# Full attention of a hybrid decoder step: scores from stacked high and low halves, a ring of two heads, six cache copies moved

## The chip, the cores and the metric

The kernel runs on one core of a Trainium2 chip. The metric is the time of one execution on the device in microseconds (us), lower is better. All data is float32 in memory. "float32r" in the profile (fp32r) is a rounded form of float32 in which TensorE works faster; a value split into a rounded high part and the rest as a low part keeps nearly all of its digits.

## The reference, cut to what matters

One layer of a decoder trunk for 1024 prompt rows and 8 x 8 sample rows. A projection gives queries, keys and values for four attentions: a full (differential) attention "B" with 4 heads, and three windowed ones. The change touches the full attention over the prompt alone, and the order of some copies of old cache rows to the output.

```python
qb = rms_norm(qb.reshape(b, s, B_HEADS, 2, HEAD_DIM), q_norm_b)      # 4 heads, 2 maps, 64 wide
kb = rms_norm(kb.reshape(b, s, B_HEADS, 2, HEAD_DIM), k_norm_b)
scores = jnp.einsum('bqhcd,bkhcd->bhcqk', q, k) * (d ** -0.5)        # c: the two maps
scores = scores - slopes[:, None, None, None] * rel.astype(jnp.float32)
p, _ = softmax_with_lse(scores, rel >= 0)                            # causal
a = p[:, :, 0] - lam * p[:, :, 1]
return jnp.einsum('bhqk,bkhe->bqhe', a, v)                           # v is 128 wide
```

## The kernel before, in words

The program is written out by hand: every engine has its own instruction list, and semaphores order them. In order of time there are 12 blocks of the input projection (kinds q, k, v for G = 0 to 3; G = 0 is the full attention B, G = 1 to 3 the windowed ones). After the three blocks of a G comes its attention over the prompt. Then come the sample rows together with the gates (902 to 1420 us), the two projections, and the output.

A block (`block_`) has nine row tiles: 8 of 128 prompt rows and one of the 64 sample rows. The weights of the next block are fetched meanwhile into a ring of four raw buffers by SyncE (SP, `load_chunk`), rounded by ScalarE (`split_hi`), and their low parts made by GpSimd (POOL, `split_lo`). `load_chunk` of a chunk waits until the one four before it has been split.

Queries and keys are normalised, stored to DRAM in 32 x 32 turned blocks, and read back as head dimension by row (`load_turned`, 16 transfers of 128 KB for each of qT and kT; those of q in the k block, those of k in the first four steps of the v block). qT and kT hold [128, 4 x 1024]: one head (64 dimensions of each map below each other) per 1024 columns.

The attention B of head h and query tile i is an element e = 8h + s, with i from TILE_ORDER (7, 0, 6, 1, 5, 2, 4, 3); it needs i + 1 key tiles. In turn:

- POOL (`scaled`): two multiplications of 64 x 128 put the scaled query of each map into its own half of qz; the other half of qz is zero (two memsets, `pad_first`), so that one product over 128 rows gives one map's scores. The first eight elements are made in the v block ahead of its second step's weight split, the others behind the scores of the element eight before.
- PE (`scores`): the product qz x kT in float32, both maps; later `probs_turn` (transposes) and `values`.
- VectorE (DVE): `biased` adds the bias table tB from PSUM and keeps the minimum; `combined` takes map 2 times lambda from map 1.
- ScalarE (ACT): `Exp`, `piece_move`, and `out_move`, which puts the result into the place of the used query in qT.
- SP: after the last weight split of the v block it loads the bias tables of heads 0 and 1 (`table_b`, since tB lies where raw does), then the tables of the later heads with four cache copies each (`tables`), and at the end four stores of 512 KB of qT to o_scr (`attention_out`).

SP issues in order: what it waits for holds back everything behind it. A cache copy (`copy_cache`, up to 2 MB) waits until the copy two before it has landed. There are 48 copies: 16 in attention B, 2 in the v block of each windowed group, 19 in the windowed attentions, 7 in the output.

## Time and profile before

| | us |
|---|---|
| median of 3 runs | 1657.69 (1652.74 to 1667.01) |
| the profiled execution's own time | 1662.27 |
| its span | 1660.3 |
| blocks of B: v block | 130 to 176 |
| attention B | 176 to 290 |
| output stage | 1550 to 1660 |

Busy time over the span: PE 1601.6 us, DVE 758.0, POOL 699.3, ACT 564.6. The profile gives start times in us from the span's start. A row of the timeline that says "x4" has merged four like instructions of an engine. A float32 matmul appears as two records, a float32r one as one. "SPq" is the issue of a transfer on SP, and its length is the time that the issue took.

### The profile page before, as it was taken

The numbers are of one execution on the slowest core, as the hardware profiler recorded it, in microseconds if no ns is written. First come the engines' busy times: TensorE is split into PE (matmuls) and PEld (weight loads), VectorE is DVE, ScalarE is ACT, GpSimd is POOL, SyncE is SP. The second block draws the span as 40 slices with busy tenths as digits, with TensorE's granted clock in tenths as the row PEclk, the third lists the DMA queues.
The fourth block names the chain that finished last, engine by engine and source line by source line (L and its number), as shares of the span: only waits on it lengthen the run. The fifth ranks groups of instructions, "written<-read, shape, count | busy, mean of one in ns | idle before, by whom it ended". The sixth has DMA issues, their size and how long they took to land.

```text
span 1660.3 us, 37307 instructions
## 1 busy us (share of the span) xinstructions
PE 1601.6 (96%) x14616; PEld 1374.4 (83%) x14616; DVE 758.0 (46%) x1852; ACT 564.6 (34%) x1341; POOL 699.3 (42%) x958
## 2 busy tenths in 40 slices
PE   6999999999999999999999999999999899999998
PEld 5787677878899999999999877778787688888787
DVE  5532577333473333733335544335454433588411
ACT  5321477121362123712136234334343234411300
POOL 5676340466533666446666112122121121675500
PEclk9999999999999999999999999999999999999999
DMA  5359896338983279933797889889988978865692
GB/s 162 112 147 189 275 310 220 102 85 155 268 274 91 83 164 255 307 104 105 169 276 246 282 304 313 276 299 324 320 297 300 306 255 248 290 199 166 206 330 95
DMA packets 351487, 369.84 MB, mean 223 GB/s; under 512 B 164113, under 2 KB 208274, under 8 KB 351314
## 3 DMA queue, kind: packets, MB, share of 16 engines
q1 hardware_dynamic: 306354, 308.55, 61.4%
q10 hardware_dynamic: 44960, 58.92, 10.6%
q8 instruction: 117, 1.92, 0.5%
q14 instruction: 56, 0.46, 0.1%
HBM read 310.83 MB, written 143.85 MB: 274 GB/s over the span
## 4 chain that ended last, share of the span: by engine, by line
PE 79%; DMA 5%; POOL 4%; DVE 4%; issue 2%; ACT 2%; SPq 1%; ACTq 1%; POOLq 0%; DVEq 0%
PE ps L2069 13%; PE ps L2071 13%; PE ps L2070 13%; PE ps L2122 4%; PE ps L2224 4%; PE ps L2123 4%; PE ps L2124 4%; PE ps L2281 4%; PE ps L2170 3%; PE ps L2244 3%; DMA v_in<-in_cache_a_kv 3%; PE ps L2342 3%; PE ps L2231 2%; PE ps L2191 2%; POOL rs L1047 2%
## 5 line engine op out<-in xcount | busy, mean ns | idle before, releaser
L1066 POOL TENSOR_TENSOR w_lo<-raw,w_hi 128x512 fp32r<-128x512 f32 x140 | 181.6, 1301 | 407.8 <-ACT w_hi L1276 407.3
L2069 PE MATMUL ps<-w_hi,hT 128*128 128x512 f32 x824 | 333.3, 405 | 2.1 <-POOL hT L1053 1.0
L2071 PE MATMUL ps<-w_hi,hT 128*128 128x512 f32 x824 | 330.0, 401 | 0.0
L2070 PE MATMUL ps<-w_lo,hT 128*128 128x512 f32 x824 | 329.8, 400 | 0.0
L2122 PE MATMUL ps<-w_hi,hT 128*128 128x256 f32 x768 | 225.6, 294 | 4.9 <-issue 4.6
L2069 PEld LDWEIGHTS ps<-w_hi,hT 128*128 128x128 f32 x824 | 206.4, 250 | 22.7 <-issue 1.4
L2071 PEld LDWEIGHTS ps<-w_hi,hT 128*128 128x128 f32 x824 | 206.0, 250 | 20.5
L2070 PEld LDWEIGHTS ps<-w_lo,hT 128*128 128x128 f32 x824 | 206.6, 251 | 19.4
L2123 PE MATMUL ps<-w_lo,hT 128*128 128x256 f32 x768 | 217.6, 283 | 0.0
L2124 PE MATMUL ps<-w_hi,hT 128*128 128x256 f32 x768 | 217.1, 283 | 0.1
L1120 POOL TENSOR_SCALAR qz<-qT,qcol 64x128 f32<-64x128 f32 x256 | 156.6, 612 | 109.6 <-PE ps L2170 54.4
L1276 ACT ACTIVATE w_hi<-raw 128x512 fp32r<-128x512 f32 x158 | 98.7, 628 | 282.7 <-DMA raw<-in_w_in 228.5
L2122 PEld LDWEIGHTS ps<-w_hi,hT 128*128 128x128 f32 x768 | 147.9, 193 | 12.0 <-issue 11.3
L2123 PEld LDWEIGHTS ps<-w_lo,hT 128*128 128x128 f32 x768 | 148.0, 193 | 1.6 <-issue 1.6
L2124 PEld LDWEIGHTS ps<-w_hi,hT 128*128 128x128 f32 x768 | 147.5, 192 | 0.0
L1796 DVE STREAM_TRANSPOSE k_in<-k_in 128x512 f32<-128x512 f32 x224 | 139.0, 678 | 5.2 <-DMA k_in<-in_cache_a_kv 2.9
L1047 POOL TENSOR_TENSOR rs<-ss,half_pow 128x8 f32<-128x8 f32 (+3 forms) x81 | 127.1, 1570 | 6.7
L1668 DVE TENSOR_TENSOR zn<-ps,rs 128x512 f32<-128x512 f32 (+1 forms) x72 | 49.8, 691 | 146.9 <-POOL rs L1047 146.9
L1386 ACT ACTIVATE sA<-sA,st_sum 128x128 f32<-128x128 f32 (+1 forms) x192 | 86.2, 449 | 59.9 <-DVE st_sum L1762 53.9
L1330 ACT ACTIVATE ps<-ps 128x512 f32<-128x512 f32 (+1 forms) x72 | 41.8, 580 | 180.0 <-PE ps L2071 171.6
L1653 DVE TENSOR_REDUCE ss<-ps 128x8 f32<-128x512 f32 (+1 forms) x72 | 49.7, 690 | 116.4 <-ACT ps L1330 116.4
L2224 PE MATMUL ps<-kT,qz 128*128 128x128 f32 (+1 forms) x384 | 100.4, 348 | 1.0 <-issue 0.8
(229 smaller groups left out, 2763.6 us busy)
## 6 DMA issues: line engine op xcount, KB each, us to landing
out<-in_cache_a_kv SPq DMA_DIRECT2D x32, 2040.0 KB, 13.9
k_in<-in_cache_b_kv SPq DMA_DIRECT2D x128, 256.0 KB, 4.3
v_in<-in_cache_b_kv SPq DMA_DIRECT2D x128, 256.0 KB, 6.3
raw<-in_w_in SPq DMA_DIRECT2D x104, 256.0 KB, 3.3
k_in<-in_cache_a_kv SPq DMA_DIRECT2D x104, 256.0 KB, 8.4
v_in<-in_cache_a_kv ACTq DMA_DIRECT2D x96, 256.0 KB, 7.2
out<-in_cache_a_kv SPq DMA_DIRECT2D x8, 2016.0 KB, 9.9
raw<-in_w_in ACTq DMA_DIRECT2D x40, 256.0 KB, 6.8
```

The source lines that it names most:

```text
L1047: return pool.tensor_tensor(out, in_, half_pow[0:r, 0:heads], ALU.pow)
L1066: pool.tensor_tensor(lo, raw_of(q), hi.bitcast(F32), ALU.subtract).then_inc(lo_done, 1)
L1120: return pool.tensor_scalar(qz[rows, half, cols], qT[rows, c * SEQ + i * P:c * SEQ + (i + 1) * P], qcol[rows, (0 if G else 1):(0 if G else ...
L1276: act.activation(weights(q)[0], raw_of(q), ACT.Copy).then_inc(hi_done, 1)
L1796: dve.transpose(k_in[:, gg % NKS, j, :], k_in[:, gg % NKS, j, :]).then_inc(s_kt, 1)
L2069: pe.matmul(z, hi, wh, start=first, stop=False)
L2070: pe.matmul(z, hi, wl, start=False, stop=False)
L2071: return pe.matmul(z, lo, wh, start=False, stop=last)
L2122: pe.matmul(part, hi, wh, start=k == 0, stop=False)
L2123: pe.matmul(part, hi, wl, start=False, stop=False)
L2124: ins = pe.matmul(part, lo, wh, start=False, stop=k == KC - 1)
L2224: pe.matmul(bank(s % 4)[:, 0:W], qz[:, hh, i * P:(i + 1) * P], kT[:, k0:k0 + W], start=True, stop=True).then_inc(aq, 1)
```

## The change

- Scores: the two products are float32r. k_hl holds, for one map of one head, the rounded keys in partitions 0 to 63 and their low parts in 64 to 127. q_hi holds the rounded query twice (in both halves), q_lo its low part twice. Scores = q_hi x k_hl + q_lo x k_hl. A piece narrower than 256 columns is widened to 256.
- For that each head and map takes 1024 columns in both halves, so qT and kT hold two heads and are a ring. One head's keys are 8 transfers of 128 KB, its queries 8 as well. Heads 0 and 1 are loaded where all four were; head h + 2 when head h has been scored, in SP's list at the fourth element of head h.
- POOL: `query_parts` (two multiplications and a subtraction of 128 x 256) replaces `scaled` for G = 0; `key_parts` (two rounds of a cast and a subtraction of 64 x 512, and a cast of 64 x 1024) is new, once per head and map. In the v block steps 1 to 4 have two `query_parts` each, steps 5, 6, 7 a `key_parts` each, all ahead of the step's weight split. The memsets of qz for G = 0 go.
- The output of B goes to a ring of four tiles, oB, and is stored per element (64 KB) by SP; `out_move` waits for the store of the element four before.
- Cache copies: 10 instead of 16 in B, 3 instead of 2 in each of three v blocks, 10 instead of 7 in the output stage.

```diff
-COPIES_B, COPIES_A = 16, ((2, 2, 2, 2), (2, 2, 2, 1), (1, 1, 1, 1))
-COPIES_V, COPIES_OUT = 2, 7
+COPIES_B, COPIES_A = 10, ((2, 2, 2, 2), (2, 2, 2, 1), (1, 1, 1, 1))
+COPIES_V, COPIES_OUT = 3, 10
...
+            def load_head(kind, part):
+                h, rest = divmod(part, 8)
+                mp, d, j = rest // 4, rest // 2 % 2, rest % 2
...
+                p0, c0 = HD * d + 32 * j, head_at(h, mp)
+                out = (kT if kind == "k" else qT)[p0:p0 + 32, c0:c0 + SEQ]
...
+            def attention_b_io():
+                more_copies(2)
+                for e in range(32):
+                    h, s = divmod(e, 8)
+                    if s == 3 and h < 2:
+                        sp.wait_ge(*scored_heads(h + 1))
+                        sp.wait_ge(bs, 16 + 16 * (h + 1))
+                        for kind, loaded in (("k", kt_in), ("q", qt_in)):
+                            sp.wait_ge(loaded, turned_in_dram(0, h + 1))
+                            for part in range(8 * h + 16, 8 * h + 24):
+                                load_head(kind, part)
+                        table_b(h + 2)
+                    sp.wait_ge(bo, 8 + e + 1)
...
+                    sp.dma_start(o_scr[0][i * P:(i + 1) * P, h * P:(h + 1) * P], oB[:, e % 4, :])\
+                        .then_inc(sig_in[e % 4], 16)
+                    if s == 4:
+                        more_copies((COPIES_B - 2) // B_HEADS)
...
+                    if kind == "v" and 0 < at_ < 5 and G == 0:
...
+                        for n in range(2 * at_ - 2, 2 * at_):
+                            query_parts(n)
+                    if kind == "v" and 4 < at_ < NT and G == 0:
+                        key_parts(0, at_ - 5) if at_ < 7 else key_parts(1, 0)
...
+            def query_parts(e):
+                h, i = e // 8, TILE_ORDER[e % 8]
+                if h:
+                    pool.wait_ge(bq, 16 + 2 * (e - 8) + 2)
...
+                pool.tensor_scalar(hi_q, raw_q, qcol[:, 1:2], None, ALU.mult)
+                link(pool.tensor_scalar(raw_q, raw_q, qcol[:, 1:2], None, ALU.mult))
+                pool.tensor_tensor(lo_q, raw_q, hi_q.bitcast(F32), ALU.subtract).then_inc(qz_ready, 1)
+
+            def key_parts(h, mp):
+                pool.wait_ge(kt_in, turned_in_dram(0, max(h, 1)))
+                pool.wait_ge(*lo_ready(last_split[0]))
+                pool.wait_ge(qz_ready, 8 * max(h, 1) + (mp if h > 1 else 0))
+                for x0 in range(head_at(h, mp), head_at(h, mp) + SEQ, CW):
+                    cols = slice(x0, x0 + CW)
+                    link(pool.tensor_copy(k_hi[HD:P, :], kT[HD:P, cols]))
+                    link(pool.tensor_tensor(k_hl[HD:P, cols], kT[HD:P, cols], k_hi[HD:P, :].bitcast(F32), ALU.subtract))
+                whole = slice(head_at(h, mp), head_at(h, mp) + SEQ)
+                pool.tensor_copy(k_hl[0:HD, whole], kT[0:HD, whole]).then_inc(h_lo, 1)
...
+                key_parts(1, 1)
+                for e in range(8, 32):
+                    h, s = divmod(e, 8)
+                    if h > 1 and s < 2:
+                        key_parts(h, s)
+                        pool.wait_ge(qt_in, turned_in_dram(0, h))
+                    query_parts(e)
...
+                    if e % 8 == 0:
+                        pe.wait_ge(h_lo, SPLIT_0 + 2 * h + mp + 1)
...
-                        w = min(CW, W - w0)
-                        ins = pe.matmul(ps[:, mp * 1024 + w0:mp * 1024 + w0 + w],
-                                        qz[:, mp, s * P:(s + 1) * P], kT[:, ds(h * SEQ + w0, w)],
-                                        start=True, stop=True)
+                        w = min(CW, max(2 * P, W - w0))
+                        z, keys = ps[:, mp * 1024 + w0:mp * 1024 + w0 + w], k_hl[:, k0 + w0:k0 + w0 + w]
+                        pe.matmul(z, q_hi[:, mp, s * P:(s + 1) * P], keys, start=True, stop=False)
+                        ins = pe.matmul(z, q_lo[:, k0 + s * P:k0 + (s + 1) * P], keys, start=False, stop=True)
```

POOL in the v block of G = 0, before (w_lo is the low part of the next block's weights, qz the padded query):

```order
L1066 TENSOR_TENSOR w_lo1_74<-raw_70,w_hi1_73 128x512
L1130 MEMSET qz_85 64x1024
L1131 MEMSET qz_85 64x1024
L1120 TENSOR_SCALAR qz_85<-qT_75,qcol_54 64x128 x16
L1066 TENSOR_TENSOR w_lo1_74<-raw_70,w_hi1_73 128x512 x7
```

Of the change, the end of the same block (k_hi is a scratch row for the rounded keys; the eight query parts of three instructions each stand ahead, two for each of the first four of these splits):

```order
L1114 TENSOR_TENSOR w_lo1_74<-raw_70,w_hi1_73 128x512
L1199 CAST k_hi_89<-kT_76 64x512
L1200 TENSOR_TENSOR k_hl_88<-kT_76,k_hi_89 64x512
L1199 CAST k_hi_89<-kT_76 64x512
L1200 TENSOR_TENSOR k_hl_88<-kT_76,k_hi_89 64x512
L1202 CAST k_hl_88<-kT_76 64x1024
L1114 TENSOR_TENSOR w_lo1_74<-raw_70,w_hi1_73 128x512
```

The 16 short multiplications stood in one run ahead of seven splits; now 24 instructions of 256 columns and three groups like this one stand between the splits, and the last split comes behind all of them.

SP from the end of the v block to the end of attention B, before (tB the bias table, out the cache copies, o_scr the stored result):

```order
L828 DMA tB_97<-in_bias_b 128x1024 x2
L818 DMA out_5<-v_sb_77 128x512
L713 DMA out_6<-in_cache_a0_kv 16x15x512
L713 DMA out_7<-in_cache_a1_kv 16x63x512
L713 DMA out_8<-in_cache_a2_kv 16x48x680 x4
L713 DMA out_6<-in_cache_a0_kv 16x15x512
L713 DMA out_7<-in_cache_a1_kv 16x63x512
L828 DMA tB_97<-in_bias_b 128x1024
```

The same place of the change:

```order
L862 DMA tB_102<-in_bias_b 128x1024 x2
L852 DMA out_5<-v_sb_77 128x512
L732 DMA out_6<-in_cache_a0_kv 16x15x512
L732 DMA out_7<-in_cache_a1_kv 16x63x512
L902 DMA o_scr0<-oB_95 128x128 x3
L795 DMA kT_76<-blocks_scr0k 32x32x32 x8
L795 DMA qT_75<-blocks_scr0q 32x32x32 x8
L862 DMA tB_102<-in_bias_b 128x1024
L902 DMA o_scr0<-oB_95 128x128 x2
L732 DMA out_8<-in_cache_a2_kv 16x48x680 x2
```

Sixteen transfers for head 2 now stand between the stores of elements 2 and 3, and the same for head 3 eight elements on.

## Rows read from the trace of the kernel before

**Rows 1.** The page's fourth part: the chain that ended last, by engine.
```profile
PE 79%; DMA 5%; POOL 4%; DVE 4%; issue 2%; ACT 2%; SPq 1%; ACTq 1%; POOLq 0%; DVEq 0%
```
**Rows 2.** Window of B's second head: length, busy PE, PEld, DVE, ACT, POOL; clock, DMA.
```profile
204.60:232.10 27.50, 27.50 (x159) 20.11 (x158) 20.79 (x57) 19.83 (x52) 10.68 (x16) 1.00 0.92 302
```
**Rows 3.** Waits from 120 to 292 us: who for whom, total, times, longest.
```profile
DVE rlB L1716 <- ACT sB L1371: 8.7, 9, 1.1
```
**Rows 4.** Timeline of PE: float32 scores, then the float32r products of a block.
```profile
204.80 1.88 PE L2170 MATMUL ps<-kT,qz 128*128 128x512 f32 x4
206.52 0.61 PE L2191 MATMUL ps<-v_sb,ptB 128*128 128x128 f32 x4
...
172.95 0.40 PE L2069 MATMUL ps<-w_hi,hT 128*128 128x512 f32 x1
173.42 0.40 PE L2071 MATMUL ps<-w_hi,hT 128*128 128x512 f32 x1
```
**Rows 5.** Groups of POOL by shape: busy us, mean ns of one, idle before.
```profile
L1120 POOL TENSOR_SCALAR qz<-qT,qcol 64x128 f32<-64x128 f32 x256 | 156.6, 612 | 109.6 <-PE ps L2170 54.4 <-PE ps L2224 39.8
L1174 POOL COPY q_rep<-qTs 32x64 f32<-32x64 f32 x128 | 29.6, 232 | 27.2 <-issue 11.2 <-PE ps L2286 10.3
L1174 POOL COPY q_rep<-qTs 32x32 f32<-32x32 f32 x128 | 26.2, 205 | 16.9 <-PE ps L2281 11.2
L1053 POOL TENSOR_TENSOR hTs<-hn,hTs 128x256 fp32r<-128x256 f32 x2 | 1.5, 733 | 2.2 <-ACT hTs L1263 2.2
L1066 POOL TENSOR_TENSOR w_lo<-raw,w_hi 128x512 fp32r<-128x512 f32 x140 | 181.6, 1301 | 407.8 <-ACT w_hi L1276 407.3
```
**Rows 6.** Timeline of POOL in the v block: start, length, instruction.
```profile
143.18 0.96 POOL L1130 MEMSET qz<- 64x1024 f32 x1
...
145.25 10.88 POOL L1120 TENSOR_SCALAR qz<-qT,qcol 64x128 f32<-64x128 f32 x16
...
169.72 1.30 POOL L1066 TENSOR_TENSOR w_lo<-raw,w_hi 128x512 fp32r<-128x512 f32 x1 [2.12 <-ACT w_hi L1276]
```
**Rows 7.** SP's issues and DVE's first bias; then landing times of tB (us).
```profile
140.21 4.37 SPq L776 DMA_DIRECT2D kT<-blocks_scr0k  x4
171.45 0.93 SPq L828 DMA_DIRECT2D tB<-in_bias_b  x2
178.23 1.22 DVE L1706 CUSTOM_DVE_ANT_0 sB<-ps,tB 128x1024 f32<-128x1024 f32 x1 [1.58 <-PE ps L2170]
...
DMA to landing us min/median/max: 4.2/7.3/14.3
```
**Rows 8.** Transfers from 120 to 292 us: count, KB, median us to landing.
```profile
kT<-blocks_scr0k SPq DMA_DIRECT2D x16, 128.0 KB, 4.4
```
**Rows 9.** Timeline: POOL beside DVE's L1723 (two SBUF inputs); its ns min/median/max.
```profile
215.94 1.15 DVE L1723 SCALAR_TENSOR_TENSOR sB<-sB,wB 128x896 f32<-128x896 f32 x1
216.09 2.15 POOL L1120 TENSOR_SCALAR qz<-qT,qcol 64x128 f32<-64x128 f32 x2 [1.58 <-PE ps L2170]
...
208.88 1.28 POOL L1120 TENSOR_SCALAR qz<-qT,qcol 64x128 f32<-64x128 f32 x2 [0.83 <-PE ps L2170]
209.72 1.29 DVE L1723 SCALAR_TENSOR_TENSOR sB<-sB,wB 128x1024 f32<-128x1024 f32 x1
...
L1723 DVE SCALAR_TENSOR_TENSOR sB<-sB,wB x32: 350/818/1290, 182.8 to 286.6; 128x1024 f32<-128x1024 f32 x4, 128x128 f32<-128x128 f32 x4, 128x896 f32<-128x896 f32 x4, 128x256 f32<-128x256 f32 x4
```
**Rows 10.** Timeline of PE: the last scores of B, and the next block.
```profile
283.49 1.02 PE L2170 MATMUL ps<-kT,qz 128*128 128x512 f32 x2
290.02 0.48 PE L2069 MATMUL ps<-w_hi,hT 128*128 128x512 f32 x1
```
**Rows 11.** Windows of PE: busy, granted clock (1.00 is 2.4 GHz), DMA share.
```profile
1016.00:1029.00 13.00, 9.10 (x218) 0.91 0.98 337
1029.00:1033.00 4.00, 4.00 (x21) 0.50 1.06 389
```
**Rows 12.** Timeline of DVE in the output stage, after the copies.
```profile
1617.77 0.69 DVE L2010 TENSOR_TENSOR yo<-ps,xl 128x512 f32<-128x512 f32 x1 [5.62 <-DMA xl<-in_x_prompt]
```

More of the change, by code:

```diff
@@ L217, in build_step @@
         qz = place("qz", [P, 2, SEQ], at=at)
+        q_hi = place("q_hi", [P, 2, SEQ], F32R, at=[work])
+        q_lo = place("q_lo", [P, NC * SEQ], F32R, at=[q_base])
+        k_hl = place("k_hl", [P, NC * SEQ], F32R, at=[k_base])
+        k_hi = place("k_hi", [P, CW], F32R, at=[work + 4 * 4 * CW])
         att = []
@@ L225, in build_step @@
                 ptB = place("ptB", [P, 4, CW], at=at)
+                oB = place("oB", [P, 4, P], at=at)
                 assert at[0] <= set_at[s] + 2 * 4 * KC * CW
@@ L598, in stored, with head_at, scored_heads, turned_in_dram @@
         def stored(G):
-            return 16 * (NC + (NC + NT) * G)
+            return 16 * (NC + NT) * G
+        def head_at(h, mp):
+            return (2 * (h % 2) + mp) * SEQ
+        def scored_heads(h):
+            return bq, 16 + 16 * h
+        def turned_in_dram(G, h=1):
+            return 256 * (G + 2) if G else 128 * (h + 1)
         def part_of(big, small, part, i):
@@ L764, in store_blocks @@
                     .then_inc(blocks_sent(G, kind, i)[0], 16)
+            def load_head(kind, part):
+                h, rest = divmod(part, 8)
+                mp, d, j = rest // 4, rest // 2 % 2, rest % 2
+                if part == 0:
+                    for i in range(NT - 2, NT):
+                        sp.wait_ge(*blocks_sent(0, kind, i))
+                base = blocks_scr[0][kind == "k"][0:1, 0:1]
+                src = bass.AP(base.tensor, base.offset + h * P + HD * mp + 32 * j, [[CW, 32], [32 * CW, SEQ // 32], [1, 32]])
+                p0, c0 = HD * d + 32 * j, head_at(h, mp)
+                out = (kT if kind == "k" else qT)[p0:p0 + 32, c0:c0 + SEQ]
+                sp.dma_start(out.rearrange("p (b r) -> p b r", r=32), src).then_inc(kt_in if kind == "k" else qt_in, 16)
             def load_turned(G, kind, part):
+                if G == 0:
+                    load_head(kind, part)
+                    return
                 c, j = divmod(part, 4)
@@ L770, in load_turned @@
                         sp.wait_ge(*blocks_sent(G, kind, i))
-                    if kind == "q" and G:
+                    if kind == "q" and G > 1:
                         sp.wait_ge(o_out, stored(G - 1))
@@ L830, in tables @@
             def tables(G):
-                if G == 0:
-                    for h in range(B_HEADS):
-                        if h >= 2:
-                            sp.wait_ge(bs, 16 + 16 * (h - 1))
-                            table_b(h)
-                        more_copies(COPIES_B // B_HEADS)
-                else:
+                if G:
                     for c in range(1, NC):
@@ L866, in attention_out @@
                         .then_inc(o_out, 16)
-                if G:
-                    sp.wait_ge(ast, 4 * G)
-                    for i in range(NT):
-                        sp.dma_start(rows_of(st_scr[G - 1], G, i), st[:, i, :]).then_inc(o_out, 16)
+                sp.wait_ge(ast, 4 * G)
+                for i in range(NT):
+                    sp.dma_start(rows_of(st_scr[G - 1], G, i), st[:, i, :]).then_inc(o_out, 16)
             for G in range(4):
@@ L875, in _ @@
                 tables(G)
-                attention_out(G)
+                attention_out(G) if G else attention_b_io()
             sp.wait_ge(av, 208)
+            for n in range(4):
+                sp.wait_ge(sig_in[n], O_STORED)
             for s in range(3):
@@ L1129, in pad_first @@
                     pool.wait_ge(k_out[s], k_sent[s][TILES * G + NT])
+            def pad_first(G):
+                zn_left(G)
                 link(pool.memset(qz[0:HD, 1, :], 0.0))
                 link(pool.memset(qz[HD:P, 0, :], 0.0))
-                pool.wait_ge(setup, 1)
-                pool.wait_ge(qt_in, 256 * (G + 1))
-                for i in range(NT) if G else TILE_ORDER:
+                pool.wait_ge(qt_in, turned_in_dram(G))
+                for i in range(NT):
                     scaled(G, 0, i, 0)
@@ L1373, in attention_b @@
                                 .then_inc(be, 1)
+                for n in range(4):
+                    act.wait_ge(sig_in[n], O_STORED)
             def attention_a(G):
@@ L1535, in halves @@
                     n = 4 * (i % 2) + 2 * br + h
-                    act.wait_ge(sig_in[n], 16 * (i // 2 + 1))
+                    act.wait_ge(sig_in[n], (O_STORED if n < 4 else 0) + 16 * (i // 2 + 1))
                     act.activation(sig[n][NS:P, :], bank(2 * br + h)[0:NS], ACT.Copy).then_inc(p_half, 1)
```

35 lines of the change are left out of this document (22 added, 13 removed).

## Prediction

> **What bounds the kernel now.** The chain of waits comes first. The reader is to see that TensorE holds 79% of it and GpSimd (POOL) 4% [rows 1]. A cut in TensorE's work counts, then, where nothing else becomes late. So I read attention B next, by a window over one head: PE is busy 27.50 of 27.50 us, DVE 20.79, ACT 19.83, POOL 10.68 [rows 2]. PE sets the pace, but DVE is only 6.7 us behind it, and POOL has 16.8 us free. The waits say what stands between DVE and its busy time: 8.7 us over four heads for ACT's exponentials [rows 3], 2.2 us per head. Without PE as the bound a head would take about 20.8 + 2.2 = 23.0 us. Last comes the timeline of POOL in the v block: it starts on the queries at 143.18 us and has split its last weights at 171.0, seven microseconds before DVE's first bias at 178.23 [rows 6, 7]. That slack is small beside what the change puts there.
>
> **PE.** Four float32 records of 512 columns take 206.52 - 204.80 = 1.72 us, 0.43 each, and a matmul has two [rows 4]: 0.86 us, or 1.68 ns per column. A head has two maps of 36 key tiles, 9216 columns: 15.5 us. A float32r product of 512 columns starts 0.235 us after the one before (0.47 for two, [rows 4]). Per map there are six pieces of 512 columns, two of 384 and four of 256 (two of them widened from 128), at 0.235, 0.176 and 0.118 us: 2.23 us, times two products and two maps, 8.9 us. I take the shorter ones in proportion. PE falls to 27.5 - 15.5 + 8.9 = 20.9 us per head. DVE's 23.0 is then later than PE, so the gain of a head, if all else keeps up, is 27.5 - 23.0 = 4.5 us, 18 us over four.
>
> **What one query part and one key part cost on POOL.** No row shows a multiplication by a column scalar at 256 columns. The row of 128 columns is 0.612 us [rows 5]. From below, 128 more columns cost what copies pay (0.232 - 0.205 us for 32 columns, 0.84 ns each): 0.72 us. From above, all of it grows with the columns: 1.22 us. In between lies the slope of the subtraction, (1.301 - 0.733) / 256 = 2.2 ns: 0.89 us. I take 0.80, since the subtraction reads two inputs and this reads one. Sixteen such instructions took 10.88 us, 0.68 each, so each has 0.07 us around it [rows 6]. A query part is 2 x 0.87 + 0.733 = 2.5 us (2.3 to 3.3). Before it was 2 x 0.68 = 1.4 us.
>
> A key part: two casts of 512 columns, two subtractions of 512, one cast of 1024, with some 0.08 us for each of five waits. A cast has no row; at the slope of copies 0.232 + 448 x 0.84 ns = 0.61 us and 1.04 us, at the slope of the subtraction 1.3 and 2.5. Subtractions are 1.30 [rows 5]. I take 2 x 0.61 + 2 x 1.30 + 1.04 + 0.4 = 5.3 us (5.0 to 7.8), since a cast reads one input as a copy does.
>
> The Trainium skill (GPSIMD Engine Reference, section 3.1) gives 1.8 cycles of 1.2 GHz per element as the best of a tight loop, 1.5 ns. No run here shows it. By it the multiplication would be 0.612 + 128 x 1.5 ns = 0.80 us, an estimate from that page.
>
> **The start of attention B.** POOL begins at 143.2 as now (the memsets went, their waits stayed). To its last split it has eight query parts, three key parts and seven splits: 20.0 + 15.9 + 7 x 1.30 = 45.0 us, so 188.2 instead of 171.0. The last split holds SP's bias table, since the table lies where the raw weights do. The table's issue takes about 0.5 us and the quickest landing was 4.2 us [rows 7]: DVE starts at 192.9 instead of 178.2. PE has the first element's scores by then and stands. Late: **+14.7 us**.
>
> **POOL within the attention.** Head 0 goes at DVE's pace and is scored about 22 us on, at 215. Only then may SP load head 2, since the ring holds two heads. Four such transfers took 4.37 us to issue [rows 7], 1.1 each; eight keys need 9 us and 4.4 us to land [rows 8]: 228. The queries land at 237. POOL meanwhile has key part (1,1), made before DVE starts, and the query parts of head 1, each behind a score of head 0; it is done by 218 and waits. From 228: key part to 233.3, queries landed at 237, a query part to 239.5, the second key part to 244.8, seven query parts to 262.3. Head 3's transfers start when head 1 is scored (about 238) and are in by 260, so they hold nothing. A key part, query part, key part and seven query parts more: 292.9. That is 30.6 us of POOL per head against 23 of DVE, so from head 2 on POOL is the bound.
>
> Then the neighbour. When DVE's L1723 ran from 215.94 to 217.09 and POOL began at 216.09, two multiplications took 2.15 us instead of 1.28, 0.87 more. When POOL was first (208.88 to 210.16) and DVE began at 209.72, DVE took 1.29 us, no more than usual (the longest of its 32 is 1.290) [rows 9]. So POOL stands while such an instruction runs, unless it was already on its way. With POOL always busy each of the 16 elements of heads 2 and 3 costs it between 0 and the median 0.82; I take 0.45, 7.2 us: 300.1. From the last scores to the next block is 290.0 - 283.5 = 6.5 us [rows 10]: attention B ends at 306.6, before it was 290.0. **+16.6 us**.
>
> The Trainium skill (SBUF — State Buffer, section "Who interferes with whom") says that a DVE instruction with two SBUF inputs and a GpSimd one that reads SBUF share a read port, and that whoever is second "fully blocks". For POOL the trace agrees, with 0.87 us. For DVE it does not at 209.72. By the rule alone DVE would lose some 0.4 us per element as well, 3 us a head.
>
> **Edits that I cost at nothing or nearly.** The per-element stores (64 KB) come under the attention, and the last replaces a 512 KB one. Six copies less in B take DMA time that PE did not wait for. The third copy in each v block comes behind the kT transfers, beside PE's products; if it held them, a windowed attention would start some us late (bounds 0 to 3 each, I take 0). In the output stage seven copies already made DVE wait for xl until 1617.77, 5.6 us [rows 12]; three banks of z hide about 11 us of that, PE showed no gap. Three more copies of some 2 us excess each bring it to the brink: +1 (0 to 6).
>
> **The sum.** 16.6 + 1 = 17.6 us. The profiled execution's own time is 1662.27 (span 1660.3), 4.6 above the median 1657.69. Its sum is 1679.9; for the median I say 1657.7 + 17.6 = 1675.
>
> About 1% (16.6 us, to 1641.1 or 1674.3) is what a measurement of this kernel can tell from no change.
>
> **The rivals.**
> - *POOL at its upper prices* (3.3 and 7.8 us). The v block ends 8 x 0.8 + 3 x 2.5 = 13.9 us later, heads 2 and 3 cost 16 x 0.8 + 4 x 2.5 = 22.8 more: 1712, or 1695 to 1705 for one price of the two. For it: 128 columns took 0.61 us where a copy of 64 took 0.23. Against: a part of that is surely fixed. 0.12.
> - *SP's list as a new wait.* Sixteen issues of 1.1 us stand between the stores of elements 2 and 3, 18 us. `out_move` of element 7 wants store 3, and it comes five elements (14.4 us) after the scores that release the transfers; with 2 us to land ACT stands about 6 us, DVE and PE behind it, twice. For it: the issues in the v block were that slow. Against: in heads 2 and 3 POOL is later anyway, so one of two counts: 1681. 0.10.
> - *The shared port blocks DVE too.* This is the rule named above, as a mechanism of this kernel: POOL is busy nearly all the time, and L1723 stands behind it for 0.4 us in each of the first eight elements, which put off head 2's transfers: +3 us, 1678. For it: POOL was rarely busy so far. Against: 209.72. 0.08.
> - *Late start and quicker pace cancel.* Both POOL prices at their lower ends without port waits: 2.5 us earlier start, 16 x 0.2 + 4 x 0.3 + 7.2 = 11.6 us less in heads 2 and 3: 1661. 0.12.
> - *POOL keeps up: faster.* The place is POOL's list in heads 2 and 3, the price that of a query part. If multiplications are fixed cost alone (0.61 us) and casts as cheap, a query part is 2.0 and a key part below 4 us, so a head costs POOL 24 and less. It decides from 23 us per head on: then DVE sets the pace. The start is 14.7 - 8 x 0.5 - 3 x 1.3 = 6.8 us late and four heads win 18 us, 26 if DVE no longer waits for ACT: 1657.7 + 6.8 - 18 = 1646, down to 1638. For it: POOL had 16.8 us free per head [rows 2]. Against: subtractions do grow with the columns [rows 5]. 0.18, two thirds of it beyond 1%.
>
> The clock is no case of its own, but it widens all of them: after 4 us of idle PE within 1016 to 1029 the granted clock of the next 4 us was 0.50, that is 1.2 GHz [rows 11]. PE will stand some 9 us at the start of B and up to 8 us ahead of head 3; each costs it perhaps 2 us, which DVE's or POOL's pace covers for the most part.
>
> **How the numbers follow.** The forecast has 0.40: POOL is the bound of B and its start is late, 1675. Its own range is 1663 to 1690: 12 less with port waits and prices low, 15 more with a query part of 3.0. Half of its chance lies above 1674.3. Slower by over 1%: 0.21 of it, 0.12, 0.08 of the third, 0.05 of the fourth, 0.46. Faster by over 1%: two thirds of 0.18, 0.12. Within 1%: the rest, 0.42. The range leaves out most of the upper end of the first rival and the lowest third of the last: 1643 to 1703.
>
> **What would show it.** In the changed profile: score products of 512 columns about 0.235 us apart; POOL's multiplications of 256 columns near 0.80 us and casts near 0.61; the last split at about 188 and the first L1706 at about 193; in heads 2 and 3 POOL busy nine tenths and more, with PE and DVE waiting for q_lo or k_hl; the next block's first product at about 307. I am wrong if the first bias comes before 185, if PE's waits in heads 2 and 3 are for st_sum alone, or if PE waits longest for a DMA.

## The result, and the profile after

| | before | after |
|---|---|---|
| median of four runs (us) | 1659.45 | 1695.8 |
| lowest to highest | 1652.74 to 1667.01 | 1693.16 to 1699.77 |
| the profiled execution, its span | 1662.27, 1660.3 | 1699.77, 1698.0 |

The ratio is 1.022 (95% interval 1.019 to 1.025): slower, as forecast, but by 36 us where I had 17.6. Medians in this text are over all executions of a kernel, but for the last kernel of experiment 10: of its four executions one took 6581.6 us, and the median is that of the other three.

A table of stages says where. The entries are starts of PE's instructions in the profiled executions (us).

| PE starts | before | after | shift |
|---|---|---|---|
| first product behind attention B | 290.0 | 320.2 | +30.2 |
| windowed attention G = 1 | 437.0 | 469.4 | +32.4 |
| windowed attention G = 2 | 652.1 | 684.1 | +32.0 |
| windowed attention G = 3 | 859.4 | 891.6 | +32.2 |
| sample stage | 921.6 | 959.4 | +37.8 |
| last score of the sample stage | 1386.5 | 1423.4 | +36.9 |
| end of the span | 1660.3 | 1698.0 | +37.7 |

So 30 us arise in B, 2 behind it, 6 in the windowed attention of G = 3. The first view is again the chain of the page. PE has fallen from 79% [rows 1] to 69%, and transfers have risen from 5% to 8%:

```profile
PE 69%; DMA 8%; DVE 3%; SPq 3%; issue 3%; POOL 2%; ACT 2%; ACTq 0%; DVEq 0%; POOLq 0%
```

Next the second and third of B's four heads (heads 1 and 2 of the text), as windows (length, busy PE, PEld, DVE, ACT, POOL; clock, DMA). Against [rows 2] the heads take 37.5 and 37.7 us instead of 27.5, no engine is busy throughout, and POOL has become the busiest, with 33.0 us in the third head:

```profile
215.70:253.23 37.53, 25.00 (x151) 21.86 (x150) 23.69 (x58) 19.79 (x53) 25.53 (x28) 0.86 0.93 196
253.23:290.96 37.73, 25.36 (x158) 22.41 (x157) 23.48 (x56) 19.71 (x53) 32.97 (x35) 0.86 0.86 195
```

The products themselves became as quick as forecast: here four float32r scores of 512 columns 0.23 us apart (compare [rows 4]), and below the end of B. The next block starts 7.0 us behind the last score, before it was 6.5 us [rows 10]:

```profile
215.93 0.47 PE L2263 MATMUL ps<-k_hl,q_hi 128*128 128x512 f32 x1
216.24 0.40 PE L2264 MATMUL ps<-k_hl,q_lo 128*128 128x512 f32 x1
216.47 0.39 PE L2263 MATMUL ps<-k_hl,q_hi 128*128 128x512 f32 x1
216.70 0.39 PE L2264 MATMUL ps<-k_hl,q_lo 128*128 128x512 f32 x1
...
313.20 0.40 PE L2264 MATMUL ps<-k_hl,q_lo 128*128 128x512 f32 x1
...
320.17 0.48 PE L2158 MATMUL ps<-w_hi,hT 128*128 128x512 f32 x1
```

The waits from 176 to 346 us name what is new (who for whom, total, times, longest). ACT now waits for stores of `oB`: four times inside B, once behind it.

```profile
DVE rlB L1805 <- ACT sB L1458: 33.3, 17, 7.2
ACT oB L1445 <- DMA o_scr<-oB: 25.5, 4, 7.9
DVE sB L1795 <- DMA tB<-in_bias_b: 16.0, 1, 16.0
ACT ps L1416 <- DMA o_scr<-oB: 14.1, 1, 14.1
POOL k_hi L1199 <- DMA kT<-blocks_scr0k: 9.9, 2, 8.9
```

The last row but one is ACT at the first Square of the next block; DVE waits for ACT there for 18 us. The row on DVE and ACT, 8.7 us in [rows 3], is 33.3, since what ACT waits is passed on to DVE. ACT's five waits one by one (timeline of ACT, the wait in brackets):

```profile
234.87 0.37 ACT L1445 ACTIVATE oB<-ps,rlB 128x128 f32<-128x128 f32 x1 [4.65 <-DMA o_scr<-oB]
248.64 0.37 ACT L1445 ACTIVATE oB<-ps,rlB 128x128 f32<-128x128 f32 x1 [7.90 <-DMA o_scr<-oB]
272.70 0.37 ACT L1445 ACTIVATE oB<-ps,rlB 128x128 f32<-128x128 f32 x1 [5.08 <-DMA o_scr<-oB]
286.44 0.37 ACT L1445 ACTIVATE oB<-ps,rlB 128x128 f32<-128x128 f32 x1 [7.87 <-DMA o_scr<-oB]
...
334.95 0.58 ACT L1416 ACTIVATE ps<-ps 128x512 f32<-128x512 f32 x1 [14.13 <-DMA o_scr<-oB]
```

And SP's own list at that place. The first wait has its cause here: a store that was due stands behind sixteen transfers of head 2 and a table, from 215.85 to 230.6. The second has it in the two copies (2 MB each) issued at 231.62, since the stores of the next elements are issued behind them: the store issued at 232.99 landed at 248.6, 0.2 us after the second copy (248.4), and ACT went on at 248.64:

```profile
213.93 0.32 SPq L902 DMA_DIRECT2D o_scr<-oB  x1
215.85 7.39 SPq L795 DMA_DIRECT2D kT<-blocks_scr0k  x8
223.28 6.40 SPq L795 DMA_DIRECT2D qT<-blocks_scr0q  x8
229.72 0.91 SPq L862 DMA_DIRECT2D tB<-in_bias_b  x1
230.67 0.90 SPq L902 DMA_DIRECT2D o_scr<-oB  x2
231.62 1.33 SPq L732 DMA_DIRECT2D out<-in_cache_a_kv  x2
```

The 32 stores of 64 KB took, from issue to landing:

```profile
DMA to landing us min/median/max: 1.5/3.9/15.8
```

My theory for the experiments had, then, two causes for late stores: their place in SP's list, and copies ahead of them. The rival was that POOL's list is the bound whatever the stores do.

### The profile page after: what moved, and what is told of

The parts are those of the page before. It is cut to its first block, busy times and chain, and to the rows that moved or that the text cites. A ratio compares the mean times of both kernels' runs of the same rounds, so it can differ in the third digit from the quotient of the medians.

```text
span 1698.0 us, 37488 instructions
## 1 busy us (share of the span) xinstructions
PE 1592.3 (94%) x14616; PEld 1383.7 (81%) x14616; DVE 762.2 (45%) x1852; ACT 563.8 (33%) x1341; POOL 782.4 (46%) x1028
## 4 chain that ended last, share of the span: by engine, by line
PE 69%; DMA 8%; DVE 3%; SPq 3%; issue 3%; POOL 2%; ACT 2%; ACTq 0%; DVEq 0%; POOLq 0%
PE ps L2158 11%; PE ps L2159 11%; PE ps L2160 11%; PE ps L2211 4%; PE ps L2213 4%; PE ps L2212 4%; PE ps L2316 4%; PE ps L2374 4%; PE ps L2336 3%; PE ps L2435 3%; DMA o_scr<-oB 3%; DMA v_in<-in_cache_a_kv 3%; PE ps L2323 2%; PE ps L2418 2%; SPq L795 2%
## 5 line engine op out<-in xcount | busy, mean ns | idle before, releaser
L2158 PE MATMUL ps<-w_hi,hT 128*128 128x512 f32 x824 | 332.9, 404 | 4.3 <-DVE zn L1757 1.9
L2158 PEld LDWEIGHTS ps<-w_hi,hT 128*128 128x128 f32 x824 | 205.9, 250 | 25.7 <-DVE zn L1757 2.4
L1177 POOL TENSOR_SCALAR qz<-qT,qcol 64x128 f32<-64x128 f32 x192 | 115.3, 600 | 42.9 <-PE ps L2316 30.8
L1094 POOL TENSOR_SCALAR ss<-ss 128x8 f32<-128x8 f32 (+3 forms) x81 | 15.9, 196 | 192.5 <-DVE ss L1742 173.5
```

The source lines that it names most:

```text
L1177: return pool.tensor_scalar(qz[rows, half, cols], qT[rows, c * SEQ + i * P:c * SEQ + (i + 1) * P], qcol[rows, 0:1], None, ALU.mult)
L2158: pe.matmul(z, hi, wh, start=first, stop=False)
```

## The experiments

All start from the changed kernel, but for the one on the kernel before. Ratios are to executions of the kernel before that were measured beside the experiment. "B ends" is the first product of the next block.

**1. Eight of the ten copies in attention B left out.** The kernel doesn't make them anywhere else, so a part of the cache is missing from its output.

```diff
-                    if s == 4:
-                        more_copies((COPIES_B - 2) // B_HEADS)
```

> The changed kernel without the eight cache copies that SP issues inside attention B (two after element 4 of each head); these eight pieces of the cache are not written at all. Theory (the ring of four output tiles is the bound in head 3, and it is late for two reasons: loads ahead of the store in SP's list, and copies ahead of the store on the DMA engines): ACT's two stalls of 7.9 us before L1445 go, the other two (4.65 and 5.08 us) stay, ACT's 14.1 us at the end of B become 4 or less; attention B ends at 309 to 313 instead of 320.2, the time is 1685 to 1689. Rival 1 (POOL's lists for heads 2 and 3 are the bound and the ring only fills time that would be waited anyway): B ends at 318 or later, time 1694 to 1697. Rival 2 (the stores land late because small packets are slow in themselves): the four stalls stay at their sizes.

**2. The stores on ACT's queue.** The function below is called one element behind `out_move`; SP's loop loses its store.

```diff
+                def out_store(e):
+                    h, i = e // 8, TILE_ORDER[e % 8]
+                    act.wait_ge(bo, 8 + e + 1)
+                    act.dma_start(o_scr[0][i * P:(i + 1) * P, h * P:(h + 1) * P], oB[:, e % 4, :])\
+                        .then_inc(sig_in[e % 4], 16)
```

> The changed kernel with the 64 KB stores of attention B issued by ACT, one element after ACT has written the tile, instead of by SP. SP's list then holds loads, tables and copies only. Theory of two mechanisms: the stalls at elements 7 and 15 (4.65 and 5.08 us, loads ahead of the store in SP's list) go, the two of 7.9 us (copies on the DMA engines) stay; B ends at 312 to 318, time 1688 to 1693. Rival 1 (the list alone is the cause of all four, since the copies too are issued by SP and wait there for copies before them): all four go, B ends at 305 to 309, 1682 to 1685. Rival 2 (POOL is the bound): B ends at 318 or later, time as changed, 1694 to 1697.

**3. Both.**

> Both at once: the stores of attention B issued by ACT, and its eight cache copies left out. Theory: no stall of ACT at L1445 above 2 us; what is left is the late start (first bias at 193) and POOL's lists, which is the case that I forecast: B ends at 304 to 309, time 1680 to 1685. If DVE's pace holds instead (POOL keeps up): 192.9 + 4 x 23 + 6.5, B ends at 291 to 295, time 1667 to 1671. Rival (POOL slower than I summed, 33 us a head and more): B ends at 315 or later, 1690 and above.

Measured against 1657.59 us of the kernel before; the row of the changed kernel is that of the result above. POOL's and PE's columns are the end of POOL's last query part and the start of PE's last score.

| kernel | median, us | ratio | ACT's waits at oB | POOL done | last score | B ends |
|---|---|---|---|---|---|---|
| changed | 1695.8 | 1.022 (1.019 to 1.025) | 25.5, four times | 299.7 | 313.2 | 320.2 |
| 1 | 1675.3 | 1.010 (1.006 to 1.015) | 10.7, twice | 297.2 | 300.4 | 307.4 |
| 2 | 1685.9 | 1.016 (1.012 to 1.021) | 0 | 297.5 | 299.7 | 306.9 |
| 3 | 1676.9 | 1.012 (1.007 to 1.017) | 0 | 298.5 | 300.7 | 307.9 |

The landing times of the stores in 1 and in 2:

```profile
DMA to landing us min/median/max: 1.5/1.6/4.1
```

```profile
DMA to landing us min/median/max: 1.5/3.5/8.5
```

Three things follow. First, one cause taken away is worth as much as both: 12.3 to 13.3 us in B. In run 1 ACT still waits twice, 10.7 us in all, and that costs nothing. The two causes do not add up, since behind them lies the same next bound. Second, that bound is POOL's list: it ends at 297 to 300 us in all four kernels, stores late or not, for it needs only scores of eight elements earlier. In the changed kernel the last score comes 13.5 us behind POOL, in the others 2 to 3. That POOL's work sets this end is not shown by these runs alone; run 8 below takes some of it away. Third, the same stores beside the same copies take 15.8 us at most on SP's queue and 8.5 on ACT's. A part of the delay is thus the shared queue; another is the load of copies (4.1 us at most in run 1, without the eight). In run 1 B ended 2 us ahead of my theory's 309 to 313. For run 2 my theory was wrong: it had the two stalls of 7.9 us stay, but all four went, as its first rival said. A ring of four tiles covers landings of 8.5 us; what stalls ACT is a store issued on SP's queue behind other transfers, whether loads or copies. Of two rivals, small packets that are slow in themselves are out (1.6 us median in run 1), and so is POOL as the only bound.

The medians scatter beyond this. Run 1 is 10 us quicker than run 2 at the same end of B; of that 6.1 us is the windowed attention of G = 3 (38.6 us against 44.7), which run 1 reaches eight copies behind, so that other pieces of the cache fall there (see run 5). The sample stage took 456 to 465 us in the profiled executions of the study without any edit there. In run 3, which leaves out the same copies, G = 3 took 37.4 us. So B is judged by its end in the profile, not by the median.

**4. The third copy in each v block.**

```diff
-COPIES_V, COPIES_OUT = 3, 10
+COPIES_V, COPIES_OUT = 2, 13
```

> The changed kernel with two instead of three copies in each v block of the windowed attentions and thirteen instead of ten in the output stage. Theory (the third copy delays the table of the windowed attention of G = 3, for which DVE waits 4.1 us, and TensorE's clock falls to 0.57 behind that): the products of that attention take 37 to 38 us instead of 43.8, time 1689 to 1691, and up to 3 more if the output stage has no room for thirteen. Rival (that attention is longer for another reason, such as the shifted stages): 43 to 44 us stay, time 1695 to 1699.

Measured: 1698.8 us, 1.024 (1.020 to 1.029). The attention of G = 3 took 37.3 us, as the theory said, and all of that was given back at the end: from the last score of the sample stage to the end of the span 281.8 us instead of 274.6 (273 to 277 in all versions with ten copies there). The time alone would have told "no effect"; the stages show +7.2 and -6.5. The profiled execution was even 7.3 us shorter than the changed kernel's, but only because its sample stage took 456.4 us instead of 464.0, within the scatter of that stage. In the output stage DVE waited for xl 50.8 us, 34.8 in the changed kernel and 11.1 before, and PE now waited 1.9 us for DVE at L2158, which it had not.

**5. The copies alone, in the kernel before.**

```diff
-COPIES_B, COPIES_A = 16, ((2, 2, 2, 2), (2, 2, 2, 1), (1, 1, 1, 1))
-COPIES_V, COPIES_OUT = 2, 7
+COPIES_B, COPIES_A = 10, ((2, 2, 2, 2), (2, 2, 2, 1), (1, 1, 1, 1))
+COPIES_V, COPIES_OUT = 3, 10
-                        more_copies(COPIES_B // B_HEADS)
+                        more_copies((3, 3, 2, 2)[h])
```

> The kernel before with nothing but the copies moved as in the changed kernel: ten in attention B (3, 3, 2, 2), three in each v block, ten in the output stage. Theory (the third copy of the v block makes the first tables of the windowed attention of G = 3 late, whatever attention B does): that attention takes 43 to 44 us instead of 37.4, those of G = 1 and G = 2 stay at 62 and 50, the output stage is 0 to 2 us longer; time 1.0035 to 1.0055 times the kernel before. Rival (the six microseconds came only from the shift of the later stages against the copies, or from the slower attention B): G = 3 stays at 37 to 39 us and the time within 0.1%.

Measured: 1665.6 us over ten runs, 1.005 (1.003 to 1.0075). G = 3 took 43.3 us instead of 37.4, G = 1 and G = 2 as before, B ended at 289.7. The waits of that stage show the same row as in the changed kernel, absent before:

```profile
DVE sA L1762 <- DMA tA<-in_bias_a: 4.5, 1, 4.5
PE ps L2231 <- DVE ptA L1772: 4.0, 1, 4.0
```

The moved copies alone thus cost the 6 us. It isn't the third copy as such, though: runs 1 and 3 keep it and took 38.6 and 37.4 us. The cache is copied in a fixed order, five pieces of 2 MB and a small one of 480 KB in turn, so moving copies also changes which pieces fall into a v block. The next table is issued 1.3 us behind the stage's first product in every kernel; the pieces in the block go with when it lands and with the length of the stage:

| pieces in the v block of G = 3 | kernels | table landed behind the first product | length of the stage |
|---|---|---|---|
| one large, one small | before, run 4 | 4.7, 5.0 | 37.4, 37.3 |
| two large, one small | runs 1, 3 | 10.2, 9.0 | 38.6, 37.4 |
| two large | run 10, both | 10.4, 10.2 | 38.7, 38.6 |
| three large | changed, runs 2, 5 to 9 | 12.9 to 14.4 | 42.7 to 44.7 |

In the v block of G = 2 of the changed kernel three large pieces cost next to nothing (50.6 us for 50.2), so the place counts too; no run moves size and place apart.

Behind such a gap of PE the granted clock is low. These are the windows of the changed kernel (columns as above): PE busy 5.5 of 8 us, then 0.57, a mixture of the levels 1.2 and 2.4 GHz:

```profile
896.00:904.00 8.00, 5.54 (x47) 5.03 (x45) 3.66 (x22) 4.38 (x21) 7.02 (x13) 1.00 1.02 367
904.00:912.00 8.00, 6.78 (x34) 6.54 (x34) 4.25 (x27) 4.38 (x20) 3.69 (x7) 0.57 0.99 334
```

**6. The wait behind B.** ACT's wait for the last stores goes from the end of `attention_b` to the place ahead of the next block's first split.

```diff
+                    if u == 3 and at_ == 0:
+                        for n in range(4):
+                            act.wait_ge(sig_in[n], O_STORED)
                     if at_ < KC:
                         split_hi(u + 1, at_)
```

> The changed kernel with ACT's wait for the last stores of attention B moved from the end of B to the place ahead of the next block's first split, behind that block's first Square. Theory: ACT's 14.1 us wait at its first Square goes and with it the 2.2 us by which the first windowed attention starts later after B than before (149.2 us from the next block's first product to it, 147.0 in every version without a long wait there); B itself ends at 320 as in the changed kernel; time 1693 to 1694.5. Rival (the 2.2 us are those of the first split, which waits for the stores either way, since its weights lie where the tiles do): 149 us stay, time 1695 to 1697.

Measured: 1698.0 us, 1.025 (1.022 to 1.028): no gain. From B's end to the attention of G = 1 it is 147.0 us, as expected (149.2 in the changed kernel), but B ended at 322.3, two later than in the changed kernel, with stalls of 26.9 us instead of 25.5. Whether the 2.2 us behind B would be won with B's end at 320 is not settled by one profile; they are also gone (147.0) in runs 1 to 3, with the wait in its old place and at most 8 us long.

**7. The order of POOL's work at the start.** With ACT's stores, four query parts and the keys of head 0 ahead of the last split, the rest behind it.

```diff
-                        for n in range(2 * at_ - 2, 2 * at_):
-                            query_parts(n)
-                    if kind == "v" and 4 < at_ < NT and G == 0:
-                        key_parts(0, at_ - 5) if at_ < 7 else key_parts(1, 0)
+                        query_parts(at_ - 1)
+                    if kind == "v" and 4 < at_ < 7 and G == 0:
+                        key_parts(0, at_ - 5, 4)
...
-                key_parts(1, 1)
+                for e in range(4, 8):
+                    query_parts(e)
+                key_parts(1, 0, 8)
+                key_parts(1, 1, 8)
```

> Stores by ACT as in e2_act_stores, and POOL's list in the v block in another order: four query parts and the two key parts of head 0 beside the splits, the other four query parts and the key parts of head 1 behind the last split. The amount of work is the same. Theory (SP's bias table waits for the last split, and a later start of B also makes POOL wait for head 2's keys, 9.2 us in e2_act_stores): the last split ends at 172.5, the first bias comes at 177 to 178 instead of 192, POOL no longer waits for keys; B is then bound by POOL's list alone from 142 us on and ends at 288 to 296 instead of 306.9; time 1667 to 1675 (e2_act_stores 1685.9). Rival (the start only moves the wait: POOL's query parts of head 0 and 1 come late for PE, or DVE and POOL hold each other up more as both are always busy): B ends at 300 or later, time 1679 or more.

Measured: 1681.1 us, 1.015 (1.010 to 1.020). The first bias came at 181.5 (191.6 in run 2), but B ended at 303.1, only 3.8 us earlier: the theory missed it, and the rival's numbers hold (300 or later, 1679 or more). The last split ended at 177.5 and not at 172.5: between 148 and 163 us POOL now waited 4.2 us for ACT's halves and 1.3 us for keys, and ACT waited 32.8 us for raw weights from 130 to 180 us, so part of the start seems bound by the transfers of weights. From there POOL never paused, and its turns from head 2's first cast (223.6) to head 3's (259.2) took 35.6 us. I had 30.6 and 3.6 for the port.

**8. The second multiplication left out,** with ACT's stores.

```diff
-                link(pool.tensor_scalar(raw_q, raw_q, qcol[:, 1:2], None, ALU.mult))
```

> Stores by ACT as in e2_act_stores, and the second multiplication of each query part (qT<-qT,qcol, 0.92 us) left out: the low query part is then made from unscaled queries, so the scores of attention B are not the reference's. Theory (POOL is the bound of heads 2 and 3 once the ring of stores is no longer late, and sets the start): eight multiplications less ahead of the last split, 7.6 us, and 16 less in heads 2 and 3, 15 us: first bias at 184 to 186, B ends at 284 to 288 instead of 306.9, time 1663 to 1668. Rival (heads 2 and 3 are bound by something else, such as the landing of their transfers or DVE and ACT behind each other): only the start counts, B ends at 298 to 301, time 1677 to 1681.

Measured: 1671.7 us, 1.009 (1.006 to 1.011). First bias 185.2, POOL done at 279.1 instead of 297.5, B ended at 294.0: 12.9 us won, between theory and rival. That POOL bounds B in run 2 is thereby shown. But POOL was done 18.4 us earlier, and 5.5 us of that met the next bound: B ended 15 us behind POOL (9 in run 2). At heads 2 and 3 POOL waited 12.0 us for keys (9.2 in run 2), so the ring of two heads (scored, sixteen transfers, two key parts) now took 26.8 and 27.8 us per head.

**9. The first multiplication on ACT.** As run 7, and `q_hi` of heads 1 to 3 written by ACT, both key parts of a head ahead of its query parts.

```diff
-                pool.tensor_scalar(hi_q, raw_q, qcol[:, 1:2], None, ALU.mult)
+                if h:
+                    pool.wait_ge(ew_ready, e - 7)
+                else:
+                    pool.tensor_scalar(hi_q, raw_q, qcol[:, 1:2], None, ALU.mult)
```

> e7_parts_later with the first multiplication of the query parts of heads 1 to 3 (q_hi<-qT,qcol, 0.92 us and 0.07 between, 24 times) done by ACT instead of POOL, two to six elements ahead, and both key parts of heads 2 and 3 ahead of their query parts. Theory (with stores by ACT and an early start, POOL's list alone sets B: 35.6 us from head 2's keys to head 3's): POOL needs 10.6 + 8 x 1.8 + 3 for the shared port = 28 us a head, the same as the turn of the ring of two heads (16 issues, landing, two key parts, 27 to 28 us in e8_no_second_product); head 3's first bias comes at 258 to 263 instead of 270.1, B ends at 290 to 295 instead of 303.1; time 1668 to 1674. Rival (ACT, 2.5 to 3.5 us more per head, now holds DVE back): DVE's heads 0 and 1 take 28 us instead of 26.2, B ends at 298 or later, 1676 and above.

Measured: 1677.2 us, 1.011 (1.007 to 1.014). The rival's numbers hold. POOL was done at 286.8, yet B ended at 302.7. A window of the third head:

```profile
240.16:271.71 31.55, 24.16 (x157) 20.52 (x156) 24.59 (x56) 22.79 (x60) 26.48 (x28) 0.95 1.02 243
```

DVE is busy 24.6 us instead of 20.8 [rows 2] and ACT 22.8 instead of 19.8, and each waits for the other (DVE 3.0 us, ACT 7.4). A third wait is new: POOL waited 15.1 us in B for the halves that ACT now makes. From head to head the first biases are 26.3, 30.6 and 31.5 us apart, in run 7 26.2, 26.2 and 36.2: what the third head won, the second lost.

**10. Copies placed anew.** Run 7 with 2 + (4, 4, 3, 0) copies in B, two per v block, and run 6's edit; then run 9 with 2 + (2, 2, 4, 3) and two per v block.

> e7_parts_later with three more things: the wait for the last stores of attention B stands before the next block's first split instead of at the end of B, the copies are two at B's start, then 4, 4, 3 and 0 behind element 4 of the four heads (13 in B), and two in each v block of the windowed attentions (ten in the output stage as before it). Theory: B ends as in e7_parts_later within 2 us; ACT no longer waits 7.9 us for stores ahead of its first Square, 0 to 2 us; the windowed attention of G = 3 takes 37 to 38 us instead of 44: 6 to 9 us below e7_parts_later, time 1660 to 1667, level with the kernel before within half a per cent. Rival (13 copies in B reach the head loads and the table): B ends 4 us or more later than in e7_parts_later and the gain of G = 3 is given back.

> e12_act_high with the copies placed anew: two at B's start, then 2, 2, 4 and 3 behind element 4 of the heads (13), two in each v block of the windowed attentions. Theory: none of B's copies is under way when head 2's and head 3's transfers are issued, so B ends within 2 us of e12_act_high, unlike e10_all, where four copies stood ahead of head 3's transfers (head 3's first bias 275.1 against 270.1 in e7_parts_later); the windowed attention of G = 3 takes 37 to 39 us instead of 44. Time 5 to 8 us below e12_act_high, 1662 to 1667. Rival (it is the number of copies in B and not their place that costs): head 3's first bias 4 us or more later than in e12_act_high.

Measured: 1678.1 us, 1.012 (1.008 to 1.015), and 1675.2, 1.012 (1.0075 to 1.017), where I had 1660 to 1667 and 1662 to 1667. In the first B ended at 308.8 (303.1 in run 7), its rival. SP's timeline shows it: four copies held SP's list for 19.6 us, and head 3's keys were issued at 242.5 instead of 234.0:

```profile
222.81 19.62 SPq L732 DMA_DIRECT2D out<-in_cache_a_kv  x4
242.54 16.13 SPq L795 DMA_DIRECT2D kT<-blocks_scr0k  x8
```

In the second B ended as in run 9 (302.8) with three more copies in it, and G = 3 took 38.6 us instead of 42.7. So in B it is the place of the copies that costs, not their number. The median moved by 2 us and not by 5 to 8; that is inside the scatter named above. No version of the changed attention reached the kernel before.

## Why the prediction was right and wrong

**Right: the start.** POOL's last split was to end at 188.2 and the first bias to come at 192.9. They came at 187.9 and 191.8:

```profile
186.62 1.26 POOL L1114 TENSOR_TENSOR w_lo<-raw,w_hi 128x512 fp32r<-128x512 f32 x1
...
191.81 1.22 DVE L1795 CUSTOM_DVE_ANT_0 sB<-ps,tB 128x1024 f32<-128x1024 f32 x1 [15.99 <-DMA tB<-in_bias_b]
```

**Right in sum, wrong in parts: POOL's prices** (groups by shape: busy, mean ns of one, idle before):

```profile
L1189 POOL TENSOR_SCALAR qT<-qT,qcol 128x256 f32<-128x256 f32 x32 | 32.6, 1018 | 0.0
L1190 POOL TENSOR_TENSOR q_lo<-qT,q_hi 128x256 fp32r<-128x256 f32 x32 | 24.5, 766 | 2.7
L1200 POOL TENSOR_TENSOR k_hl<-kT,k_hi 64x512 fp32r<-64x512 f32 x16 | 23.0, 1440 | 1.3
L1199 POOL CAST k_hi<-kT 64x512 fp32r<-64x512 f32 x16 | 9.7, 608 | 11.3 <-DMA kT<-blocks_scr0k 9.9 <-POOL q_lo L1190 0.3 <-POOL w_lo L1114 0.2
L1202 POOL CAST k_hl<-kT 64x1024 fp32r<-64x1024 f32 x8 | 8.2, 1030 | 0.5
```

Casts cost what copies pay (0.61 and 1.03, as taken). The multiplication of 256 columns took 0.92 us undisturbed, not 0.80, but the second began 0.91 us after the first, without the gap that I had: a query part took 2.64 us in the v block for 2.5, a key part 5.1 for 5.3. POOL began the block at 142.2 for 143.2, and its list ended at 299.7 for 300.1. Two slips stand in the first rival: a key part at its upper prices sums to 8.1 us and not 7.8, and one of its two prices alone gives 1692 or 1694, not 1695 to 1705. The measured 1695.8 lies in that range by chance; neither price was near.

**Right, and hidden: "attention B ends at 306.6".** Runs 1 to 3 give 307.4, 306.9 and 307.9. As soon as either cause of late stores is gone, B is what I had worked out. That it fits within 1.3 us is partly luck: POOL ended 1.6 to 2.9 us earlier than my 300.1, and the last score came 2.2 to 3.2 us behind it, for which I had nothing.

**The step that failed** is what I charged for late stores: nothing in the sum, and in the rival on SP's list "in heads 2 and 3 POOL is later anyway, so one of two counts: 1681", with a chance of 0.10. The place, the two stalls (4.65 and 5.08 us, for my 6) and the pace of POOL were right. But under "Edits that I cost at nothing or nearly" the stores "come under the attention". I never asked what else stands ahead of them: the pairs of copies behind element 4 of heads 0 and 1 made two more stalls, of 7.9 us each, and four stalls are more than POOL's lateness covers. That is 30.2 us for 16.6 in B. The wait for the last stores at the end of B (14.1 us of ACT, some 2 of PE) came from the last pair of copies in the same way and had no term at all. A sign that I had given for POOL as the bound was absent: from 176 to 320 us PE never waited for q_lo or k_hl, but 25.7 us for ACT:

```profile
PE ps L2272 <- ACT ptB L1438: 25.7, 14, 6.8
```

**The second** is in the same paragraph, "bounds 0 to 3 each, I take 0", for the third copy of a v block. It measured 0 in G = 1 and 2 and 6 in G = 3, outside the bound; run 5 shows it for the moved copies without any other edit. I bounded it by what holds PE at the block's start, and I counted copies where three large pieces in that block were the condition. What came late was the table of the second pair of heads, issued behind them; DVE waited 4.1 us for it, PE 3.6 us for DVE, and behind that gap the clock was low for a while. How the 6 us divide into gap and clock no run shows. The +1 for the output stage was right with ten copies (+0.8); run 4 shows the brink, +7.2 with thirteen.

**A rival that I gave 0.08 holds in half: the shared port blocks DVE too, behind some instructions of POOL.** Its price, +3 us, isn't seen. I had taken one DVE instruction, at 209.72 [rows 9], as evidence against it. Groups of DVE in B, first of before, then of after:

```profile
L1718 DVE SCALAR_TENSOR_TENSOR wB<-rlB,st_sum,lam 128x1 f32<-128x1 f32 x32 | 7.0, 220 | 1.1
L1723 DVE SCALAR_TENSOR_TENSOR sB<-sB,wB 128x1024 f32<-128x1024 f32 x4 | 5.1, 1286 | 0.1
```

```profile
L1807 DVE SCALAR_TENSOR_TENSOR wB<-rlB,st_sum,lam 128x1 f32<-128x1 f32 x32 | 12.1, 379 | 1.1
L1812 DVE SCALAR_TENSOR_TENSOR sB<-sB,wB 128x1024 f32<-128x1024 f32 x4 | 5.5, 1377 | 0.1
```

Even the instruction on one column takes 379 ns in the mean for 220. Over all shapes these two lines take 41.3 us for 33.1, 2 us per head. The timeline shows which of them are long. Here it begins 0.25 us into a subtraction of POOL and ends with it (at 227.63 and 227.61), and there 0.11 us into a multiplication and ends 0.43 us ahead of it:

```profile
226.34 1.27 POOL L1200 TENSOR_TENSOR k_hl<-kT,k_hi 64x512 fp32r<-64x512 f32 x1
226.59 1.04 DVE L1807 SCALAR_TENSOR_TENSOR wB<-rlB,st_sum,lam 128x1 f32<-128x1 f32 x1
...
213.77 0.92 POOL L1188 TENSOR_SCALAR q_hi<-qT,qcol 128x256 fp32r<-128x256 f32 x1
213.88 0.38 DVE L1807 SCALAR_TENSOR_TENSOR wB<-rlB,st_sum,lam 128x1 f32<-128x1 f32 x1
```

So it is in all of B in this profile: the twelve one-column instructions that began more than 0.21 us ahead of the end of a subtraction or cast of POOL all ended 15 to 18 ns behind it, and took up to 1042 ns; the six that began so within a multiplication took 219 to 375 ns. POOL's instruction at 209.72 was a multiplication, so that row was right but said nothing about the others. The Trainium skill (SBUF — State Buffer, section "Who interferes with whom") says that whoever comes second waits; the trace agrees for POOL [rows 9] and for DVE behind subtractions and casts, but not for DVE behind multiplications. In the changed kernel I see no cost of it. In run 9 the two lines take 45.5 us, but 45.3 in run 7 as well, so they don't explain why run 9 gained nothing over it.

## What to carry to other kernels

A small store that frees a ring is a link of the critical chain: ask for its place in the issuing list and for the transfers already on its queue, and give it a queue of its own if large copies share the one it has. Two stalls behind which the same next bound lies do not add, so removing one may be worth as much as removing both; remove each alone and both together before pricing them. Count copies by their bytes and by what is issued behind them, not by their number. Compare stages of the profile and not only end times: an edit can win 6.5 us in one stage and lose 7.2 in another, and the total calls it nothing.

## What the runs showed of the hardware that I had not expected

- Stores of 64 KB landed after 1.5 us at best; beside 2 MB copies the slowest took 15.8 us on the copies' queue and 8.5 us on another engine's; with eight copies of B left out the slowest took 4.1.
- A GpSimd multiplication by a column scalar took 612 ns at 128 columns [rows 5] and 0.92 us at 256.
- DVE's operation on a single column was stretched from 220 to as much as 1042 ns when it met a GpSimd subtraction or cast under way, ending 15 to 18 ns behind it; within a GpSimd multiplication it took at most 375 ns.
- Behind PE's wait of 3.6 us the granted clock over the next 8 us was 0.57, much as in [rows 11]; a table 4.1 us late went with an attention of G = 3 that was 6 us longer.
